# Hybrid decoder layer: factor sums after the sixth group, a new VectorE order in up chunk 1, earlier FFN2 loads, fewer units split before the first LayerNorm

## The reference, cut to what matters

```python
def swiglu(x, wg, wu, wd):
    return (jax.nn.silu(x @ wg) * (x @ wu)) @ wd

def reference(x, ...):                     # x is 1 x 256 x 2048, one layer
    h = x
    h = layer_norm(DN_ALPHA * h + 0.5 * swiglu(h, ffn1_wg, ffn1_wu, ffn1_wd), ln1_g, ln1_b)
    mix = token_mixer(h, w_in, conv_dw, ..., w_conv_out, w_attn_out, w_out)   # attention and convolution
    h = layer_norm(DN_ALPHA * h + mix, ln2_g, ln2_b)
    h = layer_norm(DN_ALPHA * h + 0.5 * swiglu(h, ffn2_wg, ffn2_wu, ffn2_wd), ln3_g, ln3_b)
    return h
```

## Time and profile before

| | us |
|---|---|
| median of 3 runs | 2175.01 (2174.42 to 2176.0) |
| the profiled execution, its own time | 2173.46 |
| its span in the trace | 2171.7 |
| PE busy | 2136.9 (98%) |
| DVE busy | 1734.4 (80%) |
| ACT busy | 1310.4 (60%) |
| chain that ended last: PE | 95% |

### The profile page before, as it was taken

The page is one execution under the profiler, slowest core; times in us unless marked ns, Lnnn a source line. Parts: engine busy times, 40 slices in busy tenths (PEclk is TensorE's granted clock), DMA queues, the critical chain, the costliest instruction groups (busy, mean ns, idle before and its releaser), DMA issues.

```text
span 2171.7 us, 25619 instructions
## 1 busy us (share of the span) xinstructions
PE 2136.9 (98%) x9556; PEld 1771.3 (82%) x9556; DVE 1734.4 (80%) x1438; ACT 1310.4 (60%) x1303; POOL 169.9 (8%) x281
## 2 busy tenths in 40 slices
PE   8999999999999999999999999998999999999997
PEld 6888888888887888888888888886888888888886
DVE  7799999999977567677776465658899999999986
ACT  5677777777752544454545344434677777777761
POOL 0111111111010000000000000000111111101110
PEclk9999999999999999999999999999999999999999
DMA  8688888888764555555455555555678888898862
GB/s 349 233 289 273 272 268 282 264 284 298 259 242 146 203 205 172 173 185 186 153 173 192 193 196 188 217 204 203 232 233 272 269 269 293 289 301 276 291 249 85
DMA packets 97372, 508.17 MB, mean 234 GB/s; under 512 B 13440, under 2 KB 13824, under 8 KB 56704
## 3 DMA queue, kind: packets, MB, share of 16 engines
q1 hardware_dynamic: 81216, 433.50, 54.0%
q0 software_dynamic: 16064, 73.42, 15.4%
HBM read 493.23 MB, written 13.63 MB: 233 GB/s over the span
## 4 chain that ended last, share of the span: by engine, by line
PE 95%; DVE 2%; DMA 1%; ACT 0%; issue 0%; SPq 0%; POOL 0%; DVEq 0%; ACTq 0%
PE acc L1635 11%; PE acc L1634 11%; PE acc L1633 11%; PE acc L1696 11%; PE acc L1698 11%; PE acc L1697 11%; PE tb L1698 9%; PE tb L1697 9%; PE tb L1696 9%; PE tb L1681 1%; DMA g_raw<-in_groups 1%; DVE g_lo L1030 1%; DVE act_sb L1296 0%; DMA raw<-in_stream 0%; PE tb L1957 0%; PE tb L1971 0%
## 5 line engine op out<-in xcount | busy, mean ns | idle before, releaser
L1030 DVE TENSOR_TENSOR g_lo<-g_raw,g_hi 128x2048 fp32r<-128x2048 f32 x370 | 837.9, 2284 | 120.9 <-ACT g_hi L637 120.3
L637 ACT ACTIVATE g_hi<-g_raw 128x2048 fp32r<-128x2048 f32 x370 | 706.5, 1916 | 263.1 <-PE acc L1698 82.8
L1007 DVE TENSOR_TENSOR w_lo<-raw,w_hi 128x1024 fp32r<-128x1024 f32 x272 | 326.9, 1220 | 170.7 <-ACT w_hi L597 167.3
L597 ACT ACTIVATE w_hi<-raw 128x1024 fp32r<-128x1024 f32 x272 | 279.0, 1057 | 165.0 <-PE acc L1635 99.4
L1633 PE MATMUL acc<-w_hi,xT_hi 128*128 128x512 f32 x768 | 302.2, 393 | 0.0
L1635 PE MATMUL acc<-w_hi,xT_lo 128*128 128x512 f32 x768 | 299.4, 390 | 0.0
L1634 PE MATMUL acc<-w_lo,xT_hi 128*128 128x512 f32 x768 | 299.2, 390 | 0.0
L1696 PE MATMUL acc<-g_hi,xF_hi 128*128 128x512 f32 x696 | 273.3, 393 | 15.4 <-DVE g_lo L1383 9.1
L1697 PE MATMUL acc<-g_lo,xF_hi 128*128 128x512 f32 x696 | 272.0, 391 | 0.0
L1698 PE MATMUL acc<-g_hi,xF_lo 128*128 128x512 f32 x696 | 272.0, 391 | 0.0
L1696 PE MATMUL tb<-g_hi,xF_hi 128*128 128x512 f32 x568 | 221.0, 389 | 0.0
(11 more groups left out here) (148 smaller groups left out, 2866.1 us busy)
## 6 DMA issues: line engine op xcount, KB each, us to landing
g_raw<-in_groups SPq DMA_DIRECT2D x262, 1024.0 KB, 7.0
raw<-in_stream SPq DMA_DIRECT2D x272, 512.0 KB, 4.4
g_raw<-in_groups POOLq DMA_DIRECT2D x48, 1024.0 KB, 8.0
bounce<-h_sq POOLq DMA_DIRECT2D x44, 256.0 KB, 4.9
h_in<-bounce POOLq DMA_DIRECT2D x176, 64.0 KB, 2.7
ln_gb<-in_ln SPq DMA_DIRECT2D x6, 1024.0 KB, 5.3
g_raw<-in_groups SPq DMA_DIRECT2D x4, 512.0 KB, 7.6
res<-in_x_rows SPq DMA_DIRECT2D x1, 2048.0 KB, 16.4
```

The source lines that it names most:

```text
L597: act.activation(w_hi[:, seg.split(j)], raw[:, seg.raw(j)], ACT.Copy).then_inc(hi_ready, 1)
L637: act.activation(g_hi[:, n % RING], source[:], ACT.Copy).then_inc(g_hi_ready, 1)
L1007: dve.tensor_tensor(w_lo[:, s], raw[:, seg.raw(j)], f32(w_hi[:, s]), ALU.subtract).then_inc(lo_ready, 1)
L1030: dve.tensor_tensor(g_lo[:, n % RING], source[:], f32(g_hi[:, n % RING]), ALU.subtract).then_inc(g_lo_ready, 1)
```

## The change

1. **Factors.** In the rest of chunk 0 (x4 to x7) `factors` ran behind x4 and `factors_lo` behind x6 for all four sums. Now `factors` runs behind x5, S1's low part behind x7, and the other three low parts in chunk 1 behind P2. TensorE waits for them ahead of P5 and of P6. In FFN2 `factors` first rebuilt two input blocks from high and low parts (two adds, line 1234); now ScalarE copies them from PSUM during the norm (`keep_raw`, four copies).
2. **VectorE in chunk 1** of both FFNs has another order (below): the weight sums T2 and T3 and `gate_rows` come later.
3. **Loads of FFN2's first two groups** are issued ahead of the mixer's last units, into slots 4 and 5. The last six loads of an FFN get fixed slots, so that slots 0 and 1 come free earlier. `ga` of chunk 1 is held until D3.
4. **Before the first LayerNorm** VectorE splits two units of the next part ahead of the third row sums and the other two in the norm, where it split four ahead of the last rows.

```diff
-FIRST_LOADS = {..., "ga": "u3", ...}
+FIRST_LOADS = {..., "ga": "D3", ...}
+FIRST_SUMS = ("T1", "T2", "T3", "T4")
@@ slots
-            free = {x: n - SLOTS for n, x in enumerate((0, 1, 4, 5, 2, 3))}
+            free = {x: n - SLOTS for n, x in enumerate((4, 5, 0, 1, 2, 3) if f else (0, 1, 4, 5, 2, 3))}
+                if k >= end - SLOTS:
+                    x = k - (end - SLOTS)
@@ block.sync
             load_gb(1, ln_gb[1])
-            loads(mix_out, 1)
-            sp.wait_ge(lo_ready, mix_out.unit(ND - 1, UD))
             for k in range(K1, K1 + 2):
                 load_group(k)
+            loads(mix_out, 1)
             sp.wait_ge(unit_used, mix_out.unit(ND - 1, 0))
+            sp.wait_ge(lo_ready, mix_out.unit(ND - 1, UD))
             for k in range(K1 + 2, K1 + 4):
                 load_group(k)
@@ block.scalar, plain_block_rest
-                    if g == 6:
-                        factors_hi(f)
+                factors_hi(f)
@@ block.vector, first_block
                 lo_group(f, b, "P1", "qa")
-                half_sums_before(f, b)
+                load_done(f, b, "ra")
+                split_done(f, b, "P1")
+                add(qa, qa, ra)
                 lo_group(f, b, "P5", "qa")
-                second_half_sum(f, b)
                 lo_group(f, b, "P2", "ga")
+                factors_lo(f, 1, 4)
+                lo_group(f, b, "u1", "rb")
+                load_done(f, b, "ua")
+                split_done(f, b, "P5")
+                add(qa, qa, ua)
+                lo_group(f, b, "P6", "qa")
+                lo_group(f, b, "u3", "ub")
+                dve.wait_ge(t_ready, G.sum_no[f, b, "T1"])
+                add(ra, ra, ua)
+                lo_group(f, b, "P7", "ra")
                 gate_rows(f, 0)
-                lo_group(f, b, "u1", "rb")
-                lo_group(f, b, "P6", "qa")
-                fourth_half_sum(f, b)
-                lo_group(f, b, "u3", "ub")
-                lo_group(f, b, "P7", "ra")
                 lo_group(f, b, "P3", "ua")
                 lo_group(f, b, "g1", "qb")
+                fourth_half_sum(f, b)
                 hidden_lo(f, 0)
@@ block.vector, tail
                 for c in range(ND - 1):
+                    if f == 0 and c == ND - 2:
+                        lo(conv_in, 0, 0, 1)
                     rows_out(f, c)
@@ block.vector, plain_block_rest
-                    if g == 4:
+                    if g == 5:
                         factors(f)
-                    if g == 6:
-                        factors_lo(f)
+                factors_lo(f, 0, 1)
@@ block.tensor
+                pe.wait_ge(x_lo, 8 + 4 * f)
                 product_group(f, b, "P5", W, S1, begin=True)
...
+                pe.wait_ge(x_lo, 11 + 4 * f)
                 product_group(f, b, "P6", X, S2)
...
-                pe.wait_ge(x_lo, 11 + 4 * f)
+                pe.wait_ge(s_made, 4 * f + 4)
                 fill(tb[:, BY])
```

More of the change, by code:

```diff
@@ L79 @@
               "D3": "D3", "gb": "P2b", "ga": "P2a", "D4": "D4"}
-FIRST_LOADS = {"qa": "P4", "ra": "P7", "ua": "P3", "ga": "u3", "rb": "u1", "ub": "u3", "qb": "g1", "D3": "D3", "gb": "g3",
+FIRST_LOADS = {"qa": "P4", "ra": "P7", "ua": "P3", "ga": "D3", "rb": "u1", "ub": "u3", "qb": "g1", "D3": "D3", "gb": "g3",
                "D4": "D4"}
@@ L131, in __init__ @@
                     rows += 1
-                for name in FULL_SUMS if is_full(b) else HALF_SUMS:
+                for name in FULL_SUMS if is_full(b) else FIRST_SUMS if b == 1 else HALF_SUMS:
                     sums += 1
@@ L151, in slots @@
         for f in range(2):
-            free = {x: n - SLOTS for n, x in enumerate((0, 1, 4, 5, 2, 3))}
-            for k in range(self.begin[f][1], self.begin[f + 1][1]):
+            free = {x: n - SLOTS for n, x in enumerate((4, 5, 0, 1, 2, 3) if f else (0, 1, 4, 5, 2, 3))}
+            end = self.begin[f + 1][1]
+            for k in range(self.begin[f][1], end):
                 x = min(free, key=lambda y: free[y])
+                if k >= end - SLOTS:
+                    x = k - (end - SLOTS)
                 where.append(x)
@@ L608, in block_hi, with after_norm @@
                 act.activation(dst, tb[:, bank].rearrange("p (b n) -> p b n", b=BLK), ACT.Copy).then_inc(lhs_hi, 1)
-            def after_norm(t0, ahead, dst_hi):
+            def after_norm(t0, ahead, dst_hi, keep=None):
                 def piece_hi(n):
@@ L614, in piece_hi, with keep_raw @@
                     block_hi(dst_hi(p, t), 2 * t + p % 2, t0 + n + 1)
+                def keep_raw(n):
+                    t, p = NORM_ORDER[n]
+                    if keep:
+                        act.wait_ge(lhs_lo, b_ln2 + n + 1)
+                        act.activation(keep(p, t), tb[:, 2 * t + p % 2].rearrange("p (b n) -> p b n", b=BLK),
+                                       ACT.Copy).then_inc(s_raw, 1)
                 ahead(0)
@@ L620, in after_norm @@
                 ahead(2)
+                keep_raw(0)
                 piece_hi(2)
+                keep_raw(1)
                 piece_hi(3)
+                keep_raw(2)
                 ahead(3)
+                keep_raw(3)
                 piece_hi(4)
@@ L992, in up_ahead @@
                     g_split(n2 + g, g_raw[slot_of[k2 + g]])
-            after_norm(t_ln2, up_ahead, lambda p, t: piece(p, t)[0])
+            after_norm(t_ln2, up_ahead, lambda p, t: piece(p, t)[0],
+                       lambda p, t: raw_F[:, (S2, S3)[t], GK * p:GK * (p + 1)])
             ffn(1)
@@ L1231, in factors @@
                 else:
-                    dve.wait_ge(lhs_lo, b_ln2 + 8)
-                    for n, s_n in ((A11, S2), (A21, S3)):
-                        dve.tensor_tensor(raw_F[:, s_n], f32(xF_hi[:, n]), f32(xF_lo[:, n]), ALU.add).then_inc(s_raw, 1)
-                    dve.wait_ge(s_raw, 2)
+                    dve.wait_ge(s_raw, 4)
                     x11, x21 = raw_F[:, S2], raw_F[:, S3]
@@ L1245, in factors, with factors_lo @@
                 dve.wait_ge(s_made, m + 4)
-            def factors_lo(f):
-                for n, s_n in enumerate((S1, S3, S2, S4)):
+            def factors_lo(f, first, last):
+                for n, s_n in enumerate((S1, S3, S2, S4)[first:last], first):
                     dve.wait_ge(x_hi, 7 + 4 * f + n + 1)
@@ L1318, in norm @@
                 finish_stats(0, last_rows(0), ND)
+                ahead(5)
                 dve.wait_ge(gb_loaded, 32 * (n + 1))
@@ L1321, in norm @@
                 norm_pieces(0, (0, 1), gb)
+                ahead(6)
                 piece_lo(0)
@@ L1393, in conv_ahead @@
             def conv_ahead(n):
-                lo(conv_in, 0, *((0, 1, 2, 3), (4,), (5,), (6,), (7,))[n])
+                lo(conv_in, 0, *((), (4,), (5,), (6,), (7,), (2,), (3,))[n])
             def to_xT(p, t):
@@ L1560, in up_ahead @@
             def up_ahead(n):
-                for g in ((0, 1), (2,), (), (3,), ())[n]:
+                for g in ((0, 1), (2,), (), (3,), (), (), ())[n]:
                     g_lo_of(n2 + g, g_raw[slot_of[k2 + g]])
@@ L1897, in turn_piece @@
                     pe.wait_ge(lhs_lo, b0 if n < 4 else b0 + n - 3)
+                if r0 == 10 and n >= 4:
+                    pe.wait_ge(s_raw, n - 3)
                 turn(2 * t + p % 2, [res[:, t, p * COLS + k * P:p * COLS + (k + 1) * P] for k in range(BLK)])
```

1 line of the change is left out of this document (added).

## The result

| | before | changed |
|---|---|---|
| median, us | 2175.47 (6 runs, 2174.42 to 2176.09) | 2193.26 (6 runs, 2192.22 to 2194.94) |
| ratio, 95% interval | | 1.0083 [1.0072, 1.0093] |
| the profiled execution, us | 2173.46 | 2193.73 |
| its span, us | 2171.7 | 2191.9 |

The changed kernel is 17.8 us slower. The forecast was 11.8 slower, 2186.8 us, with a range up to 2192.0: the direction and the mechanism of chunk 1 came as forecast, the size was too small, and the time lies above the range.

The account below looks back on a forecast made before the run. TensorE, busy 98% of the span, was taken as the bound, so only its waits count. 2 x 12.1 - 7.8 - 4.0 - 0.6 = +11.8 us on 2173.46, plus 1.5 to the median, gave 2186.8 us, range 2181 to 2192.

Parts of the forecast that it names:

- part 4: Chunk 1 of both FFNs: VectorE's new order makes TensorE stall twice, a loss of 12.1 us per FFN.
- the trip: Hidden values' way out to memory and back in chunk 1: taken as 12.3 us, with 8.7 and 14 as ends.
- The clock: TensorE at half clock after each wait over 3 us: a loss of 1.5 to 2.8 us, 2.1 in the middle.
- Part 1: FFN2's factor sums: x5 split ahead of TensorE's need, gaining 6.3 us of waiting plus 1.5 of clock, 7.8.
- Part 2: First norm: TensorE's wait shrinks by 2.0 to 1.3 us, without the clock loss, a gain of 4.0 us.
- Part 3: Early loads: second norm's wait falls from 2.0 to 0.5 us, new 0.9 wait in the mixer, gain 0.6.
- First stall: Chunk 1 of FFN1: TensorE waits 3.5 us ahead of u1 for ScalarE's copy Z from W, behind P6's split.
- Second half of g1: Chunk 1 of FFN1: TensorE starts it at 95.3 instead of 85.3, 10.0 us late, behind ScalarE's second save.
- the end that I had set as a bound: Upper end for the trip in chunk 1: 14 us.
- From profile to median: Whole kernel: the median taken as 1.5 us above the profiled execution's forecast of 2185.3 us.
- The trip is longer and the clock loss full: Rival for chunk 1: 14 and 2.8 us, 14.5 per FFN, 16.6 in all, 2191.6 us; chance 0.07.
- The other side: Rival: chunk 1's chain ends in time, TensorE waits nowhere there, -12.4 us, 2162.6 us; chance 0.07.

Follow-up runs that it names:

- e1: Changed kernel with VectorE's old order of chunk 1 and all four low parts in the plain chunk: 2167.86 us, ratio 0.9961.
- e8: Kernel before with the factor part alone, all four low parts in the plain chunk: 2172.46 us, ratio 0.9984.
- e10: Kernel before with the fixed slots and early loads alone: 2173.31 us, ratio 0.9988.
- e9: Kernel before with the first norm's part alone, fewer units split ahead of it: 2176.23 us, ratio 1.0005.
- e3: Changed kernel with ScalarE's copy of bank Z moved ahead of P6's split in chunk 1: 2189.54 us, ratio 1.0062.
- e5: Changed kernel with the sum T2 moved forward on VectorE to right behind P5's low part: 2186.55 us, ratio 1.0045.
- e6: Changed kernel with the third group of FFN1's tail in slot 5 instead of slot 0: 2190.46 us, ratio 1.0070.
- e11: Changed kernel with ScalarE's second save moved ahead of the split of the hidden values: 2192.95 us, ratio 1.0074.
- e12: Kernel before with VectorE's new order of chunk 1 alone, without the factors' low parts in it: 2198.23 us, ratio 1.0104.
- e7: e1 with three low parts behind u1's, T4 behind P7's, FFN2's first two groups loaded behind the mixer's units: 2163.43 us, ratio 0.9944.

## Why the prediction was wrong

**The steps that failed.** Two terms of part 4's sum were too small: the trip, taken as 12.3 us, took 13.7 in FFN1 and 14.4 in FFN2, and the clock loss behind the second stall, taken as 2.1, was 2.8 in FFN1 (2.2 in FFN2). Together chunk 1 lost 14.3 and 14.2 us instead of twice 12.1, +4.3. And a term was put at nothing: the tail of FFN1, whose loads I did not follow on the changed slots, lost 2.2. The first alone would have stayed inside the range; the tail, with smaller misses in parts 2 and 3, took the time out of it.

**The clock** (one loss of 1.5 to 2.8 per wait over 3 us, 2.1 in the middle). Too simple. The second stall was followed by half clock for 5.7 us in FFN1 and 4.5 in FFN2, and the first stalls, which I had counted without a loss of their own, by 3.4 us each, a loss of 1.7. In chunk 1 that first loss is hidden: what sets g1's second half is the chain on the other engines, so only the loss behind the last stall counts in full, 0.7 and 0.1 more than I took.

**Part 1** (7.8 gain): 8.0, right. But I followed VectorE's lead only as far as P5. With all four low parts in the plain chunk, as in e1 and e8, it is used up at P2 and u1, and 4 us are given back.

**Part 2** (4.0 gain): 3.6 (a wait of 1.75 where I had 1.3), near in size and half right in cause. The working named both the slots and the units; e10 gives the slots 3.1 alone, and e9 shows that the fewer units without the slots are no gain.

**Part 3** (0.6 gain): the wait at the column block was 1.16 (forecast 0.9), the second norm's 0.72 (forecast 0.5).

```profile
1423.33 0.49 PE L1656 MATMUL acc<-w_hi,oT_hi 128*128 128x512 f32 x1 [1.16 <-DVE res L1295]
```

In the lags the two come to +0.1 instead of -0.6. What the fixed slots do to the end of FFN1 once `ga` is held until D3, I did not follow: six loads behind one slot, a trip of 19.1 us and a wait of 1.87. This is the step that was missing altogether, +2.2.

**Part 4** (12.1 loss, twice): the mechanism step by step as forecast, and 14.3 and 14.2 in size. First stall 3.5 forecast, 3.29 and 3.30 measured. Second half of g1 10.0 late by forecast, 11.5 and 11.9 measured without the lag before the chunk. In FFN1 the gate rows ended 1.2 later than worked out (81.2, not 80.0; the start's 1.1 is in that), and the trip took 13.7 and not 12.3. In the six kernels with late gates (changed, e3, e5, e6, e11, e12) the trip took 13.7 to 14.3 us in FFN1 and 14.1 to 14.5 in FFN2: the end that I had set as a bound was the value, and the 12.3 was estimated from a trip at another place in the stream of loads. The rest is the clock. Inside it lies a wait that I did not see: the first save overwrites memory that the first write reads, so ScalarE stood 5.92 us for `bounce` and TensorE 1.13 for the save.

**From profile to median** I added 1.5. The changed kernel's profiled execution lies 0.5 above its median, the one of before 2.0 below; so of +20.3 between the two profiles +17.8 is left between the medians. Two stretches of the profile of before can be held against kernels that have the same code there. At the second norm e8 and e9, which load FFN2's first groups as it does, lose 2.8 us against it: ScalarE splits the second group from 1466.7 on in both, and from 1465.26 on in that profile, TensorE waits 3.65 and 3.70 instead of 2.03, and half clock follows, which that profile doesn't have there. At the first norm it was the other way: e8's wait of 3.28 is followed by half clock for 3.4 us, where that profile has 5.7, and e8 gains 0.9 with nothing changed there. In e8 the two differences come to 1.9, about the 2.0 by which the profile of before lies under its median. But e12, also with the code of before at both places, gains 1.6 at the first and loses 1.2 at the second. So luck at the norms is in that profile's time, how much stays open; beside e8 and e9 the early loads are worth more than beside that profile.

**The rivals.** "The trip is longer and the clock loss full" is nearly what happened: 14.5 per FFN by its account, 14.3 and 14.2 measured; its 2191.6 is 1.7 under the time. I gave it 0.07. The other side, a chain that ends in time, did not come: TensorE waited 3.3 us for the fork.

**The start** (+1.1) belongs to no edit: the stretch is the same in all kernels here, and the lag of the twentieth matmul varies from -0.3 to +2.4 us between them, with how the first weights arrive.

## What to carry to other kernels

When an edit reorders one engine, follow each moved step to the instruction of another engine that waits for it, and then to what stands behind that instruction in its queue; the stall appears under the name of the last in line, and moving only that one changes the name and not the time. A round trip through memory has no length of its own: it takes what the loads issued beside it leave, so time it in the place where it will run, and look what a change of buffers lets the load queue issue at once. Measure each part of a composite change alone, and the whole too: here the three other parts, with a fitting order (e7), were worth 12 us and the new order cost more than twice that; one of the three only pays with another, and one loss, in the tail, came only from two of the edits together.

## What the runs showed of the hardware that I had not expected

- The granted clock after a short wait isn't set by the wait's length alone. A wait of 3.29 or 3.30 us in front of u1 was followed by half clock for 3.4 us in the changed kernel (mean 0.70 over 5.6 us), by 0.50 over 5.6 us in e11, and in FFN2 of e6 by full clock. At the first norm it was 1.00 behind a wait of 2.33 us in e10, 0.71 over 5.6 (half clock first, then full) behind one of 2.33 us in e12, 0.50 over 5.6 behind 3.16 in the kernel before, and 0.70 over 5.6 behind 4.24 in e9. The windows of e6, e10 and e12:

```profile
1546.70:1552.30 5.60, 5.57 (x24) 1.00 0.10 12
```

```profile
684.20:689.80 5.60, 5.52 (x29) 1.00 0.01 4
```

```profile
695.60:701.20 5.60, 5.60 (x22) 0.71 0.01 2
```

  What decides between them stays open; nothing was tried on it.

- The same round trip of 0.5 MB out and back took 9.0 us with hardly a load beside it (mean DMA share 0.34, its own traffic), 10.3 at a share of 0.43, 12.3 and 13.7 in chunk 1 at 0.70 and 0.76, 13.9 at 0.78 and 19.1 at 0.91.
